# Memory attention by token tile: feed-forward weights split in quarters between its steps, with evictions, softmax steps and the norm's power in another order

## The chip, the cores and the metric

The kernel runs on one core of a Trainium2 chip. The metric is the device time of one execution in microseconds. Five engines work side by side, each through its own instruction stream in order: PE (TensorE, matmuls and transposes), ACT (ScalarE), DVE (VectorE), POOL (GpSimd) and SP (SyncE, which here only starts transfers). They wait for each other by semaphores.

## The reference, cut to what matters

The program computes two transformer blocks, of two layers each, on 256 tokens of 1024 features in float32. The change touches only the memory attention, which stands once in each of the two layers of the first block:

```
for layer in range(2):
    x = x + rms_norm(mixer(rms_norm(x, g[0])), g[1])
    q = rms_norm(x, g[2]) @ wq                     # 1024 -> 4 heads x 64
    k, v = rms_norm(mem) @ wk, rms_norm(mem) @ wv  # 256 memory tokens
    p = softmax(q k^T / 8)                         # 256 x 256 for each head
    x = x + rms_norm((p v) @ wo, g[3])             # 4 x 64 -> 1024
    h = rms_norm(x, g[4])
    x = x + rms_norm((silu(h @ wg) * (h @ wu)) @ wd, g[5])
```

The mixer of layer 0 is `even_mixer`, that of layer 1 `diff_mixer`.

## The kernel before

**Tiles.** The 256 tokens are two tiles of 128. A product with a weight is three matmuls of PE: each operand is held as a rounded high part and a low part (the rest), and high x high, high x low and low x high are added up (`three_products`, L689 to L691).

**Weights.** All weights pass as units of at most 128 x 2048 floats. SP loads a unit into one of six raw slots (`load`, L488), once the unit that held the slot is used up. `part` splits it: ACT rounds it (L521) into one of three high slots, waiting until the unit three places earlier is used; DVE subtracts (L504) and leaves the low part over the raw one. The query weight wq has a high buffer of its own ("own"), which may be written once its `opened` marks are set. `part` can work in one piece or in four quarters. `prepare` splits all that may be split; `trickle(n)` issues n steps of such a split, in quarters; `take` hands out the next unit and, with `ahead=False`, prepares only if that unit isn't whole yet. `may_part` decides: the unit three places earlier must have its last use in the program, and if `turn["gentle"]` is set, a count of filler steps must also have moved on since. In the memory attention no filler runs, so that count stands still.

**Order of the work.** The order on each engine is the order in which this Python code issues instructions. The mixer's output product `second_half` yields eight steps, tile 0 first. `memory_attention` takes six of them, begins the norm of x for tile 0 (`begin_norm`: `turn` transposes x on PE L1425, `split` evicts it with ACT L1442 and DVE L1449, four blocks for each half), takes the rest of the product, closes the mixer's sublayer (`ends`: multiply by the gain L1587, update x L1601), and then issues `norm.rest()`: the squares of x for tile 0 (ACT L1461), a small DVE step (L839) and the power on POOL (L844). Then, for each tile: queries (PE, evicted by DVE L2380 with the norm's factor and 1/8), their transposes (`turn_query`, PE L2393, evicted by ACT L2399), scores (PE L2418), maxima (DVE L2428), exponentials (ACT L2442), scaling (DVE L2453, L2458), transposes of the probabilities (`turn_probs`, PE L2473, evicted by ACT L2480 for head pair 0 and DVE L2487 for pair 1), values (PE L2503, evicted by ACT L2512 and DVE L2517), the output product by wo (`project`, two column halves), and `out_.leave`: squares (ACT L1545), their sum (DVE L1569), a power (POOL L1575), multiply (L1587), update of x (L1601). `ready.later` issues the transposes, squares, power and splits for tile 1's norm; its callback issues `turn_query(0)`, `scores(0)` and the maxima of tile 0 between them.

**Waits to know.** `turn_query` waits for DVE's latest count at its place in the program, `scores` for ACT's latest. `update of x` waits also for the latest issued squares of x.

**Hand-over.** The feed-forward (`ffn`) first takes its units f0 and f1 (gate and up weights of chunk 0, four of the eight blocks of 128 features each), multiplies tile 0 by f0, issues `ready.later` (transposes of tile 1 of x into four banks), multiplies tile 0 by f1, then tile 1 by both. f2 and f3 are chunk 1, f4 the first down weight. f2 may be rounded when wo is used up.

The first `take` of `ffn` is the only place where f0, f1 and f2 are split:

```
first = [take(ahead=False), take(ahead=False)]
for tt in range(TT):
    gate_up(0, first[0], 0, [tt])
    if tt == 0:
        ready.later(banks[4:8])
        prepare()
    gate_up(0, first[1], KD // 2, [tt])
    hidden(0, [tt])
```

## Time and profile before

| | us |
|---|---|
| median of 3 runs | 2139.26 |
| lowest, highest | 2136.69, 2139.48 |
| the profiled execution | 2141.67 |
| its span, first to last instruction | 2139.4 |
| PE busy in the span | 2039.1 (95%) |
| DVE busy | 1253.2 (59%) |
| ACT busy | 1044.2 (49%) |
| POOL busy | 140.7 (7%) |

All moments in the text are microseconds from the start of the span. The memory attention of layer 0 and the hand-over to its feed-forward lie between about 225 and 290, those of layer 1 between about 592 and 655. Matmuls are pipelined: the start of one follows the start of the last by less than its own duration.

### The profile page before, as it was taken

To read this page: it belongs to the slowest core of one execution; us is meant where nothing else is said; L and a number is where in the kernel's file an instruction comes from. 1 tells how busy PE (TensorE), PEld (TensorE's weight loads), DVE (VectorE), ACT (ScalarE), POOL (GpSimd) and SP (SyncE) were. 2 spreads that over 40 slices of the span, in tenths; PEclk is the share of its full clock that TensorE was granted. 3 is DMA by queue.
4 is the path that set the end of the run, shared out by engine and by line. 5 is a ranking of instruction groups with operands and counts; after the bars stand their busy time and mean duration, and the time that the engine had idled before them with its cause. 6 is when DMAs were issued, how large, how long until landed. Compare 5 with 4: busy or idle time off the path is not lost.

```text
span 2139.4 us, 26939 instructions
## 1 busy us (share of the span) xinstructions
PE 2039.1 (95%) x9980; PEld 1680.7 (79%) x9980; DVE 1253.2 (59%) x1872; ACT 1044.2 (49%) x1679; POOL 140.7 (7%) x146
## 2 busy tenths in 40 slices
PE   7988789999869999999999999999999999999999
PEld 7775678887758888888777788888888877878887
DVE  5546554566754556555675865545545685876444
ACT  5545454355544345444456555444443566555433
POOL 0000000000000000000312210000000221120000
PEclk9987899999989999999999999999999999999999
DMA  8430355554225555565553545555555553435552
GB/s 286 133 110 22 109 181 184 190 187 158 89 89 168 187 188 176 186 195 180 165 178 104 168 138 177 191 184 182 191 188 186 165 186 126 158 118 177 188 186 98
DMA packets 247127, 346.11 MB, mean 162 GB/s; under 512 B 26132, under 2 KB 180056, under 8 KB 247000
## 3 DMA queue, kind: packets, MB, share of 16 engines
q1 hardware_dynamic: 246168, 342.92, 49.5%
q8 instruction: 81, 1.33, 0.3%
q0 software_dynamic: 544, 1.29, 0.2%
q14 instruction: 46, 0.38, 0.1%
q10 hardware_dynamic: 288, 0.21, 0.0%
HBM read 343.32 MB, written 2.33 MB: 162 GB/s over the span
## 4 chain that ended last, share of the span: by engine, by line
PE 87%; DVE 6%; ACT 3%; issue 3%; POOL 1%; DMA 0%; ACTq 0%; DVEq 0%; POOLq 0%
PE bank L689 26%; PE bank L691 25%; PE bank L690 25%; PE bank L965 2%; DVE w_lo L504 2%; PE bank L1285 1%; ACT w_hi L521 1%; PE bank L624 1%; PE bank L1093 1%; PE bank L1425 1%; POOL gain L2659 1%; PE bank L2084 1%; PE bank L1143 1%; DVE probs L1078 1%; DVE jobstat L1012 0%
## 5 line engine op out<-in xcount | busy, mean ns | idle before, releaser
L504 DVE TENSOR_TENSOR w_lo<-raw,w_hi 128x2048 fp32r<-128x2048 f32 (+6 forms) x487 | 740.0, 1539 | 418.0 <-ACT w_hi L521 417.9
L689 PE MATMUL bank<-w_hi,h_hi 128*128 128x512 f32 (+3 forms) x1872 | 739.9, 395 | 30.2 <-DVE w_lo L504 20.4
L521 ACT CAST w_hi<-raw 128x2048 fp32r<-128x2048 f32 (+6 forms) x487 | 616.4, 1295 | 258.3 <-PE bank L691 256.8
L690 PE MATMUL bank<-w_lo,h_hi 128*128 128x512 f32 (+3 forms) x1904 | 734.3, 386 | 0.0
L691 PE MATMUL bank<-w_hi,h_lo 128*128 128x512 f32 (+3 forms) x1872 | 725.2, 387 | 0.0
L689 PEld LDWEIGHTS bank<-w_hi,h_hi 128*128 128x128 f32 x1872 | 355.9, 190 | 103.6 <-DVE w_lo L504 15.9
L690 PEld LDWEIGHTS bank<-w_lo,h_hi 128*128 128x128 f32 x1904 | 363.3, 191 | 64.1
L691 PEld LDWEIGHTS bank<-w_hi,h_lo 128*128 128x128 f32 x1872 | 355.3, 190 | 69.8
L689 PE MATMUL bank<-w_hi,ff_hi 128*128 128x512 f32 x528 | 206.4, 391 | 0.0
L691 PE MATMUL bank<-w_hi,ff_lo 128*128 128x512 f32 x528 | 205.6, 389 | 0.0
L690 PE MATMUL bank<-w_lo,ff_hi 128*128 128x512 f32 x528 | 205.5, 389 | 0.0
L1264 ACT ACTIVATE ff_silu<-bank,rs 128x256 f32<-128x256 f32 x132 | 56.4, 474 | 203.9 <-PE bank L691 203.8
L1296 ACT CAST ff_hi<-bank 128x512 fp32r<-128x512 f32 x66 | 38.8, 587 | 226.9 <-PE bank L1285 226.9
L1301 DVE TENSOR_TENSOR ff_lo<-bank,ff_hi 128x512 fp32r<-128x512 f32 x66 | 45.6, 691 | 121.5 <-ACT ff_hi L1296 121.5
L689 PEld LDWEIGHTS bank<-w_hi,ff_hi 128*128 128x128 f32 x528 | 99.1, 188 | 20.9 <-DVE ff_lo L1301 0.3
L691 PEld LDWEIGHTS bank<-w_hi,ff_lo 128*128 128x128 f32 x528 | 99.1, 188 | 20.8
L690 PEld LDWEIGHTS bank<-w_lo,ff_hi 128*128 128x128 f32 x528 | 99.1, 188 | 20.2
L1273 DVE SCALAR_TENSOR_TENSOR ff_hid<-bank,rs,ff_silu 128x256 f32<-128x256 f32 x132 | 58.4, 480 | 93.6 <-ACT ff_silu L1264 93.6
L844 POOL TENSOR_TENSOR rs<-rs,const 128x1 f32<-128x1 f32 (+3 forms) x39 | 36.0, 923 | 898.6 <-DVE rs L839 809.5
L1442 ACT ACTIVATE h_hi<-bank,cols 128x128 fp32r<-128x128 f32 x192 | 53.1, 383 | 38.5 <-PE bank L1425 38.4
L1449 DVE SCALAR_TENSOR_TENSOR h_lo<-bank,cols,h_hi 128x128 fp32r<-128x128 f32 x192 | 52.8, 344 | 15.3 <-ACT h_hi L1442 14.9
L965 PE MATMUL bank<-kT,qT 64*128 64x256 f32 (+1 forms) x320 | 44.9, 419 | 10.9 <-POOL gain L2659 7.9
(324 smaller groups left out, 1690.9 us busy)
## 6 DMA issues: line engine op xcount, KB each, us to landing
raw<-in_ffn_w SPq DMA_DIRECT2D x176, 512.0 KB, 4.7
raw<-in_w_in SPq DMA_DIRECT2D x48, 1024.0 KB, 5.3
raw<-in_ffn_w SPq DMA_DIRECT2D x44, 1024.0 KB, 4.9
raw<-in_ffn_wg SPq DMA_DIRECT2D x44, 512.0 KB, 4.0
raw<-in_ffn_wu SPq DMA_DIRECT2D x44, 512.0 KB, 5.0
raw<-in_ffn_wd SPq DMA_DIRECT2D x22, 1024.0 KB, 4.9
raw<-in_od_w_in SPq DMA_DIRECT2D x12, 1024.0 KB, 5.2
raw<-in_w_out SPq DMA_DIRECT2D x8, 1024.0 KB, 5.1
```

Of the source, the lines that this page charges most:

```text
L504: dve.tensor_tensor(lo_[:, cs], raw_[:, cs], hi[:, cs].bitcast(F32), ALU.subtract).then_inc(*dve_did.up())
L521: act.copy(hi[:, cs], raw_[:, cs]).then_inc(*act_did.up())
L689: pe.matmul(out, x_hi, u.hi[:, k, cols_], start=start, stop=False)
L690: pe.matmul(out, x_hi, u.lo[:, k, cols_], start=False, stop=False)
L691: return pe.matmul(out, x_lo, u.hi[:, k, cols_], start=False, stop=stop)
L965: mm = pe.matmul(tile(i, j, tt), l, r, start=(m == 0 and (tt == 0 or not masked)), stop=(m == len(pairs[j]) - 1 and not masked), skip_grou ...
L1264: act.activation(ff_silu[:, c % 2, tt, :], bank.t[:, 0:FF_CHUNK], ACT.Silu, scale=r(tt)).then_inc(*act_did.up())
L1273: dve.scalar_tensor_tensor(ff_hid[:, c % 2, tt, :], bank.t[:, FF_CHUNK:2 * FF_CHUNK], r(tt), ff_silu[:, c % 2, tt, :], ALU.mult, ALU.mult) ...
L1296: act.copy(ff_hi[:, c % 2, :, :], ps).then_inc(*act_did.up())
L1301: dve.tensor_tensor(ff_lo[:, c % 2, :, :], ps, ff_hi[:, c % 2, :, :].bitcast(F32), ALU.subtract).then_inc(*dve_did.up())
L1442: act.activation(h_hi[:, k0 + b, ts_], bank.t[:, b * P:(b + 1) * P], ACT.Copy, scale=gains[b]).then_inc(*act_did.up())
L1449: dve.scalar_tensor_tensor(h_lo[:, k0 + b, ts_], bank.t[:, b * P:(b + 1) * P], gains[b], h_hi[:, k0 + b, ts_].bitcast(F32), ALU.mult, ALU. ...
```

## The change

The query factor 1/8 moves from the eviction of the queries to the eviction of their transposes. For tile 0 these two evictions change engines (ACT, then DVE). `turn_query` and `scores` wait for the eviction that they need. Tile 1's transposes and scores are issued before tile 0's scaling and transposed probabilities. Four `trickle(2)` stand between the steps and `gentle` is no longer set. Both norms' `rest()` (squares and power of tile 0) are issued before the last steps of the product ahead of them. The last product of wo (`project(1, 512)`) is issued after both splits of tile 0. In layer 1, wq may be split only after the transposes of the mixer's second half. Whole diff:

```
@@ -2339,7 +2339,6 @@
             written(1)
             while "half" not in there:
                 fill()
-            own_units[1].opened = attended["o"]
             acc = out_banks()
             first_half = out_steps(acc, h_in, 0, there["half"])
             for _ in norm_steps(1):
@@ -2348,6 +2347,7 @@
             groups, steps = half_of_o(KD // 2, there["normed", 1], lambda b: cols[:, 1, c:c + 1])
             for _ in steps:
                 pass
+            own_units[1].opened = attended["o"]
             memory_keys(1)
             for _ in first_half:
                 pass
@@ -2360,7 +2360,7 @@
             W = MEM_H * HD
             PAIRS = MEM_H // 2
             kv = memory_kv[l]
-            scored, peaked, exped, scaled, copied, summed = ({} for _ in range(6))
+            queried, turned_q, scored, peaked, exped, scaled, copied, summed = ({} for _ in range(8))
             banks_of, turned_in = {}, {}
 
             def p_of(tt, j, hp):
@@ -2372,37 +2372,54 @@
                 return z[:, tt, 512 + j * 512:1024 + j * 512]
 
             def query(tt, c, n, bank, full):
+
+                if tt == 0:
+                    @block.scalar
+                    def _(act):
+                        act.wait_ge(*full)
+                        act.wait_ge(*turn["normed"][tt])
+                        act.activation(z[:, tt, 0:W], bank.t[:, 0:W], ACT.Copy, scale=rs[:, tt:tt + 1]).then_inc(
+                            *act_did.up())
+                    queried[tt] = bank.drained = act_did.now()
+                    return
 
                 @block.vector
                 def _(dve):
                     dve.wait_ge(*full)
                     dve.wait_ge(*turn["normed"][tt])
-                    dve.tensor_scalar(z[:, tt, 0:W], bank.t[:, 0:W], rs[:, tt:tt + 1], HD ** -0.5, ALU.mult,
+                    dve.tensor_scalar(z[:, tt, 0:W], bank.t[:, 0:W], rs[:, tt:tt + 1], None,
                                       ALU.mult).then_inc(*dve_did.up())
-                bank.drained = dve_did.now()
+                queried[tt] = bank.drained = dve_did.now()
 
             def turn_query(tt):
 
-                bank, ready_q, ts_ = next_bank(), dve_did.now(), slice(tt * P, (tt + 1) * P)
+                bank, ts_ = next_bank(), slice(tt * P, (tt + 1) * P)
 
                 @block.tensor
                 def _(pe):
                     pe.wait_ge(*bank.drained)
-                    pe.wait_ge(*ready_q)
+                    pe.wait_ge(*queried[tt])
                     for b in range(PAIRS):
                         m = pe.transpose(bank.t[:, b * P:(b + 1) * P], z[:, tt, b * P:(b + 1) * P], ident)
                     m.then_inc(*pe_did.up())
-
-                @block.scalar
-                def _(act):
-                    act.wait_ge(*pe_did.now())
-                    act.copy(qT[:, 0:PAIRS, ts_],
-                             bank.t[:, 0:W].rearrange("p (a b) -> p a b", a=PAIRS)).then_inc(*act_did.up())
-                bank.drained = act_did.now()
+                ps = bank.t[:, 0:W].rearrange("p (a b) -> p a b", a=PAIRS)
+                if tt == 0:
+                    @block.vector
+                    def _(dve):
+                        dve.wait_ge(*pe_did.now())
+                        dve.tensor_scalar(qT[:, 0:PAIRS, ts_], ps, HD ** -0.5, None, ALU.mult).then_inc(*dve_did.up())
+                    bank.drained = dve_did.now()
+                else:
+                    @block.scalar
+                    def _(act):
+                        act.wait_ge(*pe_did.now())
+                        act.activation(qT[:, 0:PAIRS, ts_], ps, ACT.Copy, scale=HD ** -0.5).then_inc(*act_did.up())
+                    bank.drained = act_did.now()
+                turned_q[tt] = bank.drained
 
             def scores(tt):
 
-                there, ts_ = act_did.now(), slice(tt * P, (tt + 1) * P)
+                ts_ = slice(tt * P, (tt + 1) * P)
                 for j in range(2):
                     banks_of[tt, j] = next_bank()
                     banks_of[tt, j].held = True
@@ -2411,7 +2428,7 @@
                 def _(pe):
                     pe.wait_ge(*banks_of[tt, 0].drained)
                     pe.wait_ge(*banks_of[tt, 1].drained)
-                    pe.wait_ge(*there)
+                    pe.wait_ge(*turned_q[tt])
                     for hp in range(PAIRS):
                         for j in range(2):
                             r_ = slice(j * HD, (j + 1) * HD)
@@ -2543,12 +2560,12 @@
             norm.turn()
             norm.split(0)
             norm.split(1)
+            ready = norm.rest()
             for _ in products:
                 pass
             for end in ends:
                 end()
             ends.clear()
-            ready = norm.rest()
             wq = take(ahead=False)
             pair = [next_bank() for _ in range(TT)]
             for bank in pair:
@@ -2569,46 +2586,44 @@
             queries(1)
             powers(0, 0)
             powers(0, 1)
+            turn_query(1)
             normalise(0, 0)
-            turn_query(1)
             normalise(0, 1)
+            scores(1)
+            trickle(2)
             turn_probs(0, 0)
-            scores(1)
+            peak(1, 0)
             turn_probs(0, 1)
-            peak(1, 0)
             peak(1, 1)
             powers(1, 0)
+            values(0)
             powers(1, 1)
-            turn["gentle"] = True
-            trickle()
-            values(0)
             normalise(1, 0)
             normalise(1, 1)
             turn_probs(1, 0)
-            turn_probs(1, 1)
+            trickle(2)
             for bank in banks[4:8]:
                 bank.held = True
             out_ = Sublayer(post_gain)
-            turn["gentle"] = False
             wo = take(ahead=False)
-            turn["gentle"] = True
             project(0, 0)
-            trickle()
+            turn_probs(1, 1)
+            trickle(2)
             project(0, 512)
             values(1)
-            trickle()
+            trickle(2)
             project(1, 0)
             norm = begin_norm(x, col_of[("pre", l, 4)], rs[:, 0:2])
             norm.turn()
             norm.split(0)
+            norm.split(1)
+            ready = norm.rest()
             project(1, 512)
             for end in ends:
                 end()
             ends.clear()
-            norm.split(1)
-            turn["gentle"] = False
             attended["o"] = marks()
-            return norm.rest()
+            return ready
 
         for l in range(DEPTH):
             products = (even_mixer if l % 2 == 0 else diff_mixer)(load_gain(a["sandwich_g"][l, 1, :]))
```

## Rows read from the trace of the kernel before

**Rows 1.** page, busy time over the span; then windows: PE, PEld, DVE, ACT, POOL, clock, DMA

```profile
PE 2039.1 (95%) x9980; PEld 1680.7 (79%) x9980; DVE 1253.2 (59%) x1872; ACT 1044.2 (49%) x1679; POOL 140.7 (7%) x146
...
292.00:345.00 53.00, 53.00 (x244) 43.85 (x243) 28.14 (x21) 21.82 (x20) 0.00 (x0) 1.00 0.57 180
```

**Rows 2.** timeline of the hand-over in layer 0 (start, duration, engine, line, operation)

```profile
266.31 0.60 ACT L1545 ACTIVATE sq<-bank 128x512 f32<-128x512 f32 x1 [1.41 <-PE bank L691]
...
267.89 1.42 DVE L1601 SCALAR_TENSOR_TENSOR x<-o_buf,stat,x 128x512 f32<-128x512 f32 x2
...
268.93 5.52 ACT L521 CAST w_hi<-raw 128x2048 fp32r<-128x2048 f32 x3
...
270.88 6.70 DVE L504 TENSOR_TENSOR w_lo<-raw,w_hi 128x2048 fp32r<-128x2048 f32 x3 [0.28 <-ACT w_hi L521]
...
273.27 0.76 PE L689 MATMUL bank<-w_hi,h_hi 128*128 128x512 f32 x1 [7.01 <-DVE w_lo L504]
...
278.50 1.03 PE L1425 MATMUL bank<-const,x 128*128 128x128 f32 x8
...
287.74 0.37 SPq L488 DMA_DIRECT2D raw<-in_ffn_wd  x1
```

**Rows 3.** waits from 594 to 640, the same place in layer 1

```profile
PE bank L689 <- DVE w_lo L504: 7.0, 1, 7.0
```

**Rows 4.** timeline of layer 0, from the norm to the first output product

```profile
232.68 0.48 DVE L2380 TENSOR_SCALAR z<-bank,rs 128x256 f32<-128x256 f32 x1 [0.74 <-POOL rs L844]
...
233.57 0.41 PE L2393 MATMUL bank<-const,z 128*128 128x128 f32 x2 [1.12 <-DVE rs L839]
...
234.53 1.13 PE L2418 MATMUL bank<-kT,qT 64*128 64x256 f32 x8 [0.55 <-ACT qT L2399]
...
239.52 0.48 DVE L2380 TENSOR_SCALAR z<-bank,rs 128x256 f32<-128x256 f32 x1 [1.21 <-PE bank L691]
...
242.48 1.13 PE L2418 MATMUL bank<-kT,qT 64*128 64x256 f32 x8 [0.77 <-ACT z L2480]
...
249.09 1.94 PE L2473 MATMUL bank<-const,probs 128*128 128x128 f32 x8 [2.91 <-DVE jobstat L2453]
...
251.81 0.80 PE L689 MATMUL bank<-w_hi,h_hi 128*128 128x512 f32 x1 [0.78 <-DVE z L2487]
...
260.77 0.47 PE L689 MATMUL bank<-w_hi,h_hi 128*128 128x512 f32 x1 [2.11 <-issue]
```

**Rows 5.** groups by form over the whole run: busy, mean ns | idle before

```profile
L521 ACT CAST w_hi<-raw 128x2048 fp32r<-128x2048 f32 x243 | 464.0, 1915 | 199.3 <-PE bank L691 199.3
L521 ACT CAST w_hi<-raw 128x512 fp32r<-128x512 f32 x196 | 112.8, 624 | 52.8 <-PE bank L691 52.8
...
L504 DVE TENSOR_TENSOR w_lo<-raw,w_hi 128x2048 fp32r<-128x2048 f32 x243 | 557.8, 2300 | 352.1 <-ACT w_hi L521 352.1
L504 DVE TENSOR_TENSOR w_lo<-raw,w_hi 128x512 fp32r<-128x512 f32 x196 | 134.5, 720 | 36.1 <-ACT w_hi L521 35.9
```

**Rows 6.** timeline of layer 1: end of the mixer, first query eviction, f1 used up

```profile
579.04 2.28 DVE L504 TENSOR_TENSOR w_lo<-raw,own_hi 128x2048 fp32r<-128x2048 f32 x1
581.24 1.65 DVE L680 SCALAR_TENSOR_TENSOR h_lo<-bank,cols,h_hi 128x256 fp32r<-128x256 f32 x4
...
583.00 0.47 PE L689 MATMUL bank<-w_hi,h_hi 128*128 128x512 f32 x1 [1.40 <-issue]
...
599.32 0.48 DVE L2380 TENSOR_SCALAR z<-bank,rs 128x256 f32<-128x256 f32 x1 [0.74 <-POOL rs L844]
...
653.07 0.37 SPq L488 DMA_DIRECT2D raw<-in_ffn_wd  x1
```

**Rows 7.** windows of layer 0, columns as in rows 1

```profile
247.00:249.00 2.00, 0.00 (x0) 0.00 (x0) 1.17 (x5) 0.76 (x4) 0.00 (x0) 0.68 0.00 0
249.00:257.00 8.00, 7.13 (x20) 5.40 (x20) 2.01 (x5) 1.27 (x3) 0.00 (x0) 0.50 0.00 0
...
266.00:274.00 8.00, 0.99 (x4) 0.66 (x3) 6.50 (x11) 7.70 (x11) 2.86 (x4) 0.64 0.50 151
```

More of the change, by code:

```diff
@@ L2374, in query, with _ @@
             def query(tt, c, n, bank, full):
+                if tt == 0:
+                    @block.scalar
+                    def _(act):
+                        act.wait_ge(*full)
+                        act.wait_ge(*turn["normed"][tt])
+                        act.activation(z[:, tt, 0:W], bank.t[:, 0:W], ACT.Copy, scale=rs[:, tt:tt + 1]).then_inc(
+                            *act_did.up())
+                    queried[tt] = bank.drained = act_did.now()
+                    return
                 @block.vector
@@ L2545, in memory_attention @@
             norm.split(1)
+            ready = norm.rest()
             for _ in products:
@@ L2571, in memory_attention @@
             powers(0, 1)
+            turn_query(1)
             normalise(0, 0)
-            turn_query(1)
             normalise(0, 1)
+            scores(1)
+            trickle(2)
             turn_probs(0, 0)
-            scores(1)
+            peak(1, 0)
             turn_probs(0, 1)
-            peak(1, 0)
             peak(1, 1)
             powers(1, 0)
+            values(0)
             powers(1, 1)
-            turn["gentle"] = True
-            trickle()
-            values(0)
             normalise(1, 0)
@@ L2591, in memory_attention @@
             out_ = Sublayer(post_gain)
[L2592 removed]
             wo = take(ahead=False)
[L2594 removed]
             project(0, 0)
[L2596 removed]
+            turn_probs(1, 1)
+            trickle(2)
             project(0, 512)
             values(1)
[L2599 removed]
+            trickle(2)
             project(1, 0)
@@ L2603, in memory_attention @@
             norm.split(0)
+            norm.split(1)
+            ready = norm.rest()
             project(1, 512)
@@ L2607, in memory_attention @@
             ends.clear()
-            norm.split(1)
-            turn["gentle"] = False
             attended["o"] = marks()
-            return norm.rest()
+            return ready
         for l in range(DEPTH):
```

43 lines of the change are left out of this document (23 added, 20 removed).

## The prediction, made before the changed kernel ran

> **What bounds the kernel now.** I read the page first: PE is busy 95% of the span, so time can only come from PE's idle stretches and from stretches at a low clock. In the feed-forward that follows the memory attention PE is busy 53.00 of 53 us at clock 1.00 [rows 1]: whatever the attention gains is passed on whole, and nothing can be gained there. Then the waits: the longest single wait of PE in each of the two layers is the same one, 7.0 us at the hand-over, until DVE has written a low part [rows 2, 3]. The timeline shows why. The last output product ends at 266.3. Only then are f0, f1 and f2 split, in whole units and behind the squares of x: ACT starts at 268.93, DVE at 270.88, PE at 273.27 [rows 2]. Last the timeline of the attention itself: a chain passes from PE to ACT or DVE and back, with idle PE between [rows 4], and PE's clock falls in it: 0.68 and 0.50 after the idle stretch at 247 to 249, again 0.64 around the 7 us wait [rows 7]. 12 matmuls take 5.2 us there (273.27 to 278.50) and 36 take 8.3 at clock 1.00 (279.4 to 287.7) [rows 2], so 0.43 and 0.23 each. These are the levels of 1.2 and 2.4 GHz.
>
> **The change part by part, layer 0.** I follow one chain with durations of the rows, first at clock 1.00.
>
> *Norm's power and queries.* The squares of tile 0 move ahead of the mixer's last square, into an idle ACT; their DVE and POOL steps move with them. Tile 0's query eviction waited 0.74 for POOL [rows 4]; now ACT does it when PE is done, at 231.7. Its transposes waited 1.12 for the small DVE step of tile 1 [rows 4]; they no longer do, but their eviction, now on DVE, stands behind that same step (233.4). So the first scores start at 233.8, not at 234.53, and tile 1's query eviction at 238.8, not at 239.52: 0.7 gained. Moving the factor 1/8 costs nothing: the same number of instructions on the same shapes.
>
> *Tile 1's scores.* They started at 242.48 because two copies of tile 0's probabilities and the scaling stood before them [rows 4]. Now: eviction to 239.3, transposes to 239.8, copy to 240.2, scores at 240.3. 2.2 gained in all. The next work on ACT, two quarter casts, lies in its wait for PE.
>
> *To the first output product.* From scores(1) to it went 9.3 us (242.48 to 251.81): maxima, all four exponential steps, values, the scaling, and then transposes of both head pairs (1.94) and a copy on DVE before the product could start [rows 4]. Now values(0) stands between the exponentials and the product follows the first transposes of tile 1: scores 1.1, transposes of tile 0's second head pair and their copy 1.7, values 1.2, their evictions 0.85, scaling of tile 1's first pair 0.75, its transposes 0.5, signals included: 6.1. The product starts at about 246.3, 5.5 earlier. Its bank may be one that ACT still reads until 247.1; I charge 0.8 for that.
>
> *The quarters.* A quarter cast takes 624 ns against 1915 for a whole one, a quarter low part 720 against 2300 [rows 5]. So f0 and f1 cost 8 x 0.62 = 5.0 us of ACT and 8 x 0.72 = 5.8 of DVE, one DVE quarter of it after the attention. The Trainium skill, VectorE: DVE Perf Modes, section "The TRN2 errata", speaks against splitting: instructions that read SBUF pay a fixed extra each on ScalarE and VectorE. The rows agree: four quarters cost 0.58 us of both engines more for a unit than one whole piece (2.50 - 1.92, 2.88 - 2.30) [rows 5]. On ACT all eight stand before idle time. On DVE three stand in front of the x update of tile 0 and tile 1's low values, so the idle before project(1, 0), 2.11 now [rows 4], grows to 2.9. No DMA moves but by its slot's release: f0 and f1 are in their slots before the attention.
>
> *The two orders of the last product.* project(1, 512) now ends at 257.8 instead of 266.3, 8.5 earlier (5.5 from before, 4.8 from 24 matmuls at 0.23 instead of 0.43, minus the 0.8 of longer idle and 1.0 of new short waits, for the square behind quarters and the transposes of x). What is newly late: its squares stand on ACT behind tile 0's second split and the norm's squares, 259.6 instead of 257.9. They hold the sum, POOL's power, the multiply and tile 1's update of x, there at 262.6, and so PE's transposes of tile 1.
>
> *Hand-over.* f0 is whole, so PE multiplies tile 0 at 258.8, after the split of tile 0's first half, to 261.8; waits 0.9 for x; transposes to 263.7; f1 (its last quarter done at 263.2) to 266.5; f2's four quarters stand before tile 1's splits on DVE, costing 0.5; both units for tile 1 to 272.7. Now that point is 287.7 [rows 2]. **15.0 us gained.** f2 is needed only then and is whole by 265.7.
>
> **Layer 1.** Its first query eviction is at 599.32, 366.64 after layer 0's; f1 is used up at 653.07 [rows 6], 286.4 on layer 0's scale, so 13.7 gained. Besides, the low part of wq (2.28) stands before the mixer's last h_lo, for which PE waits 1.40 [rows 6]. It moves behind: the h_lo is there at 580.8, before PE asks, **1.4 gained**. wq and wo are then whole about 10 us before use.
>
> **Sum.** At clock 1.00 throughout: 15.0 + 13.7 + 1.4 = 30.1. But by the same chain the new order still has idle stretches of PE (1.8 before 246, 2.9 before 254, 1.2 and 0.9 at the hand-over). If the clock stays low from 247.6 to 262, about as long as now [rows 7], f1 is used up at 276.3, 3.6 later in each layer: 22.9. What the new order's clock does no row shows; I take the middle, 26.5, since the longest idle shrinks only from 2.91 to about 2.9, in another place, while the one of 7.01 goes. Minus 2 x 0.8 for the bank: **24.9**. The ends: 30.1, and 11.5 with the clock low until f1 is through (below). The profiled execution took 2141.67, 2.4 more than the median of the runs, 2139.26; the sum is a difference within its span and I take it off the median: 2139.3 - 24.9 = **2114.4**.
>
> **Rivals.**
> - *Only the hand-over gains.* The quarters fill what the new order frees, and the last product ends at 266.3 as now. Then x of tile 1 comes 1.8 later than now (271.1), transposes end at 272.2 instead of 279.5: 7.3 each, 2 x 7.3 + 1.4 = 16.0, 2123. For: both engines carry the work and are strictly in order. Against: ACT is busy 1.27 of the 8 us from 249 to 257, DVE 2.01 [rows 7].
> - *The clock stays low through f0 and f1.* f1 is used up at 282.0: 5.7 + 4.4 + 1.4 = 11.5, 2127.8. For: it is low now after idle stretches, 0.50 from 249 to 257 with PE busy 7.13 of 8 us [rows 7]. The Trainium skill, TensorE: Matmul & The Clock Gate, section "What's actually happening", says that the throttled state is the default and activity releases it; by that rule a denser attention loses less clock than the present one, which would give a time nearer to 2109. The trace agrees so far that the clock is 1.00 throughout the dense feed-forward [rows 1].
> - *Slower: the quarters lie on the chain.* Seven DVE and eight ACT quarters fall where PE waits, each delaying the next step of the softmax: 5.0 + 5.0 = 10.0 us a layer, against 7.3 at the hand-over. 2 x 2.7 - 1.4 = 4.0 slower, 2143. It decides once more than 7.3 of 10.0 us is exposed and reordering gives nothing. Against it: before project(1, 0) only three DVE quarters can stand in the way, and ACT waits for PE elsewhere.
> - *The splits aren't issued.* If a unit weren't allowed by its predecessor's use, trickle would do nothing and the 7 us wait stay; the attention's reordering alone would give about 6 a layer, 2126. Against: f0's and f1's predecessors are the mixer's last two units, used before, and `gentle`, which forbade them, is off.
>
> **Chances.** Forecast 0.64, hand-over only 0.16, low clock 0.08, not issued 0.05, slower 0.04, none of these 0.03. All but the last two are faster by more than 0.2% (4.3 us, about what a measurement of this kernel can tell from no change): faster 0.92, same 0.04, slower 0.04. Range: from 2106, the 30.1 with 3 us for stretches elsewhere whose clock may fall otherwise once all is shifted, to 2127, which takes in the hand-over case and part of the low clock one.
>
> **What would show it.** Right: no cast or low part of 128x2048 at the hand-over but eight quarter casts a layer inside the attention and four after it; PE's wait for L504 at f0 gone and one of about 1 us for tile 1's x in its place; scores(1) about 2 us after tile 1's query eviction began, not 3; the first output product some 13 to 14 us after the first query eviction, not 19; layer 1's 1.40 gone. Wrong: a wait of PE on a low value behind quarters longer than 4 us before project(1, 0); clock 0.50 at f0; a whole split still at the hand-over; idle of PE in the feed-forward, where the gain would be given back.

## The result, and the profile after

The changed kernel takes 2111.01 us (median of 4 runs, 2110.32 to 2112.74) against 2139.01 of the kernel before beside it: ratio 0.9872, 95% interval [0.9855, 0.9890], 28.0 us less. The forecast was 2114.4, its range 2106 to 2127.

Two executions, one of e2 below (8310.19 us) and one of the kernel before beside e5 to e8 (7141.30), lie thousands of microseconds above the rest, and no reading uses them.

The spans of the two profiled executions, 2139.4 and 2108.4, differ by 31.0, three more than the medians: the profiled execution of before (2141.67) took 2.7 us more than the median beside it, that of the changed kernel (2110.32) 0.7 less. Most of this lies in one place outside the change, shown at the end.

The page of the changed kernel, busy time over the span (as rows 1): PE has 10.9 us less busy time with the same 9980 matmuls, so part of the gain is clock; DVE and ACT have 18 instructions more each.

```profile
PE 2028.2 (96%) x9980; PEld 1672.0 (79%) x9980; DVE 1253.8 (59%) x1890; ACT 1043.8 (50%) x1697; POOL 140.5 (7%) x146
```

Groups by form of the changed kernel (as rows 5): six units, f0, f1 and f2 of each layer, have gone from whole pieces to quarters (243 to 237, 196 to 220). The four quarters still cost 0.59 us of ACT (4 x 625 - 1913) and 0.54 of DVE (4 x 709 - 2296) more than the whole.

```profile
L504 DVE TENSOR_TENSOR w_lo<-raw,w_hi 128x2048 fp32r<-128x2048 f32 x237 | 543.3, 2296 | 350.3 <-ACT w_hi L521 350.3
L521 ACT CAST w_hi<-raw 128x2048 fp32r<-128x2048 f32 x237 | 452.5, 1913 | 199.6 <-PE bank L691 199.6
...
L504 DVE TENSOR_TENSOR w_lo<-raw,w_hi 128x512 fp32r<-128x512 f32 x220 | 148.6, 709 | 36.9 <-ACT w_hi L521 36.6
L521 ACT CAST w_hi<-raw 128x512 fp32r<-128x512 f32 x220 | 126.1, 625 | 52.3 <-PE bank L691 52.3
```

The timeline of the changed kernel, first the attention of layer 0 (as rows 4), then its hand-over (as rows 2), then layer 1 (as rows 6). Line numbers have moved: L2381 and L2390 are the query evictions of tiles 0 and 1 (before L2380), L2403 their transposes (L2393), L2410 and L2416 the evictions of these, L2435 the scores (L2418), L2470 the scaling (L2453), L2490 the transposes of the probabilities (L2473), L2534 the low part of the values (L2517).

```profile
232.37 0.47 ACT L2381 ACTIVATE z<-bank,rs 128x256 f32<-128x256 f32 x1 [2.19 <-PE bank L691]
...
234.54 1.13 PE L2435 MATMUL bank<-kT,qT 64*128 64x256 f32 x8 [1.06 <-DVE qT L2410]
...
239.24 0.48 DVE L2390 TENSOR_SCALAR z<-bank,rs 128x256 f32<-128x256 f32 x1 [1.21 <-PE bank L691]
...
240.60 1.13 ACT L521 CAST w_hi<-raw 128x512 fp32r<-128x512 f32 x2
...
240.85 1.14 PE L2435 MATMUL bank<-kT,qT 64*128 64x256 f32 x8 [0.56 <-ACT qT L2416]
...
246.71 1.09 PE L2490 MATMUL bank<-const,probs 128*128 128x128 f32 x4 [1.73 <-DVE jobstat L2470]
...
247.45 0.78 PE L689 MATMUL bank<-w_hi,h_hi 128*128 128x512 f32 x1
...
254.14 0.16 DVE L1569 SCALAR_TENSOR_TENSOR stat<-stat 128x1 f32<-128x1 f32 x1 [0.54 <-ACT sq L1545]
...
255.00 1.42 DVE L1601 SCALAR_TENSOR_TENSOR x<-o_buf,stat,x 128x512 f32<-128x512 f32 x2
256.33 0.42 DVE L2534 TENSOR_TENSOR h_lo<-bank,h_hi 128x256 fp32r<-128x256 f32 x1
...
256.85 0.47 PE L689 MATMUL bank<-w_hi,h_hi 128*128 128x512 f32 x1 [2.44 <-ACT w_hi L521]
...
261.09 1.12 ACT L1461 ACTIVATE sq<-x 128x1024 f32<-128x1024 f32 x1
...
262.13 0.66 ACT L1545 ACTIVATE sq<-bank 128x512 f32<-128x512 f32 x1
...
262.70 2.24 ACT L521 CAST w_hi<-raw 128x512 fp32r<-128x512 f32 x4
...
263.77 1.42 DVE L1601 SCALAR_TENSOR_TENSOR x<-o_buf,stat,x 128x512 f32<-128x512 f32 x2
...
264.67 1.29 PE L1425 MATMUL bank<-const,x 128*128 128x128 f32 x8 [1.10 <-DVE x L1601]
...
265.10 3.09 DVE L504 TENSOR_TENSOR w_lo<-raw,w_hi 128x512 fp32r<-128x512 f32 x5
...
274.59 0.37 SPq L488 DMA_DIRECT2D raw<-in_ffn_wd  x1
...
566.06 1.66 DVE L680 SCALAR_TENSOR_TENSOR h_lo<-bank,cols,h_hi 128x256 fp32r<-128x256 f32 x4
...
568.90 2.29 DVE L504 TENSOR_TENSOR w_lo<-raw,own_hi 128x2048 fp32r<-128x2048 f32 x1 [1.19 <-ACT own_hi L521]
```

PE no longer stops 7.0 us for a low part. f1 is used up at 274.59 instead of 287.74. No cast of 128x2048 is left at the hand-over: eight quarter casts lie inside the attention (the two shown at 240.60, and two each at 248.31, 250.98 and 254.72) and four behind it, at 262.70. In layer 1 the low part of wq now follows the mixer's last h_lo instead of standing before it.

Windows of the changed kernel, layer 0 and one later stage (columns as in rows 1): the clock still falls in the attention, but it is back at 1.00 for f0 and f1, where before it was 0.64 [rows 7].

```profile
247.00:252.00 5.00, 5.00 (x17) 4.12 (x16) 2.46 (x6) 3.23 (x7) 0.00 (x0) 0.50 0.00 0
252.00:257.00 5.00, 2.56 (x22) 1.78 (x21) 4.37 (x9) 2.20 (x6) 0.55 (x1) 0.92 0.00 0
...
262.00:270.00 8.00, 6.86 (x32) 4.96 (x32) 7.16 (x18) 7.80 (x20) 2.86 (x4) 1.00 0.85 241
...
280.00:330.00 50.00, 50.00 (x227) 41.42 (x226) 26.63 (x19) 20.83 (x18) 0.00 (x0) 1.00 0.58 190
...
1849.00:1853.00 4.00, 4.00 (x24) 3.40 (x23) 4.00 (x8) 2.98 (x6) 2.69 (x2) 1.00 0.25 98
```

In layer 1 it falls twice: it is 0.70 from 598 to 603, 1.00 in the next 4 us and 0.60 from 607 to 611.

**Where the time went.** I cut each trace at the same instructions. Attention: from the mixer's third square to the first square of the attention's own output product. Product: from there to its last square. Hand-over: from there to the second silu, when f1 is used up. Wq: in layer 1, from the last reduction of the mixer's norm to the mixer's third square. Differences of starts in the timelines, in us; the span is that of the traced execution, the median that of all (e11 is one execution):

| kernel | attention, layers 0, 1 | product | hand-over | wq | span | median |
|---|---|---|---|---|---|---|
| before | 29.9, 31.2 | 11.5, 9.0 | 21.4, 21.4 | 21.2 | 2139.4 | 2139.0 |
| changed | 24.7, 24.5 | 11.7, 11.9 | 12.5, 12.5 | 19.5 | 2108.4 | 2111.0 |
| e1 only the order | 23.1, 23.1 | 10.8, 10.9 | 19.3, 19.2 | 19.6 | 2115.8 | 2122.2 |
| e11 only the quarters | 30.8, 32.1 | 11.5, 9.1 | 13.7, 13.7 | 21.2 | 2125.0 | 2126.9 |
| e3 wq back | 23.7, 23.6 | 12.1, 12.4 | 12.5, 12.5 | 21.2 | 2109.1 | 2112.1 |
| e4 old front | 26.0, 26.0 | 11.1, 11.1 | 12.5, 12.5 | 19.5 | 2110.9 | 2115.0 |
| e10 old back | 27.0, 26.4 | 10.5, 10.5 | 12.5, 12.5 | 19.6 | 2111.0 | 2112.9 |
| e12 old front and back | 29.8, 30.6 | 10.9, 10.5 | 12.5, 12.5 | 19.5 | 2119.7 | 2119.2 |
| e5 casts twice | 24.7, 24.7 | 12.3, 12.5 | 12.5, 12.5 | 19.6 | 2109.9 | 2111.7 |
| e6 low parts twice | 24.7, 24.2 | 13.7, 13.6 | 12.4, 12.5 | 19.6 | 2114.4 | 2115.6 |
| e7 whole units | 27.6, 27.9 | 14.0, 13.0 | 12.0, 12.0 | 19.5 | 2117.9 | 2122.0 |
| e8 late rest | 23.6, 24.7 | 11.4, 10.4 | 13.7, 13.7 | 19.5 | 2108.5 | 2110.5 |
| e9 late rest, x sooner | 24.4, 24.5 | 8.2, 8.2 | 12.5, 12.4 | 19.5 | 2104.4 | 2104.7 |

In the feed-forward PE is busy 50.00 of 50 us, as before [rows 1], so nothing of the gain is given back there. The hand-over gave 9.0 and 8.9, the attention with its product 5.0 and 3.8, the mixer's end in layer 1 1.7: 28.4. The span shows 2.6 more, from stretches the change doesn't touch: 3.6 behind the second hand-over, less 1.0 ahead of the two attentions.

**How far two traces can be compared.** Layer 0 of e3 has the same instructions as layer 0 of the changed kernel, for e3 differs from it in layer 1 only. It took 48.2 us where the changed kernel took 48.9, with the attention 1.1 shorter and the product 0.4 longer. The cause is the clock, as the last section shows. So a difference of 0.7 us a layer between two traces is no more than one code shows by itself. And a traced execution needn't be a typical one: the time of an execution is 1.9 to 2.4 us above its span; so the trace of e1 is of its fastest execution, 4.1 below its median, that of e4 lies 2.3 below, and that of e12 is of its slowest, 2.5 above.

### The profile page after: what moved, and what is told of

It reads as the page before. It is cut to its first block and busy times, and to the rows that moved or that the text cites. A ratio compares the mean times of both kernels' runs of the same rounds, so it can differ in the third digit from the quotient of the medians.

```text
span 2108.4 us, 26993 instructions
## 1 busy us (share of the span) xinstructions
PE 2028.2 (96%) x9980; PEld 1672.0 (79%) x9980; DVE 1253.8 (59%) x1890; ACT 1043.8 (50%) x1697; POOL 140.5 (7%) x146
## 5 line engine op out<-in xcount | busy, mean ns | idle before, releaser
L689 PE MATMUL bank<-w_hi,h_hi 128*128 128x512 f32 (+3 forms) x1872 | 738.3, 394 | 12.1 <-DVE w_lo L504 4.7
L965 PE MATMUL bank<-kT,qT 64*128 64x256 f32 (+1 forms) x320 | 43.8, 411 | 10.9 <-POOL gain L2674 7.9
```

The lines of the kernel that those rows point to most:

```text
L689: pe.matmul(out, x_hi, u.hi[:, k, cols_], start=start, stop=False)
L965: mm = pe.matmul(tile(i, j, tt), l, r, start=(m == 0 and (tt == 0 or not masked)), stop=(m == len(pairs[j]) - 1 and not masked), skip_grou ...
```

## The experiments

### The two halves of the change

Only the order: the four `trickle(2)` are gone, and f0, f1 and f2 are split at the hand-over as before.

```
             scores(1)
-            trickle(2)
             turn_probs(0, 0)
...
             values(1)
-            trickle(2)
             project(1, 0)
```

> The changed kernel without its four trickle(2): f0, f1 and f2 are split whole at the hand-over again, everything else is the new order. If pre-splitting and order are both worth something (my theory): the last output product ends at about the same time as in the changed kernel, then PE waits some 6 us for f0's low part and has a low clock after it, about 7 us a layer more than the changed kernel's 2111: 2125, half of the whole gain. If the order is worth nothing and all of the gain is the hand-over (rival 1): 2137 or so, the layer-1 gain of the moved wq alone. If the order and the clock carry nearly all (rival 2): 2113 to 2116.

Measured: 2122.15 (2118.06 to 2122.83), ratio 0.9914 [0.9899, 0.9928]. The wait for the low part is back, 5.33 long; the timeline of e1:

```profile
259.42 5.49 ACT L521 CAST w_hi<-raw 128x2048 fp32r<-128x2048 f32 x3
...
261.74 4.49 DVE L504 TENSOR_TENSOR w_lo<-raw,w_hi 128x2048 fp32r<-128x2048 f32 x2
264.13 0.77 PE L689 MATMUL bank<-w_hi,h_hi 128*128 128x512 f32 x1 [5.33 <-DVE w_lo L504]
```

Only the quarters: the kernel before, with the four `trickle(2)` at the same steps in its own order.

```
             scores(1)
+            trickle(2)
...
-            turn["gentle"] = True
-            trickle()
             values(0)
...
             values(1)
-            trickle()
+            trickle(2)
```

> The kernel before with only the four trickle(2) put between its old steps and gentle left off: the quarters alone, in the old order. My theory: PE's 7.0 us wait goes and a wait of about 3 us for tile 1's x remains (its update ends 3 us after the product); 7 to 9 us a layer gained less 1 for quarters on the chain: 2139 - 15 = 2124. Rival 1: 2113 to 2116, since the hand-over is all. Rival 2, or quarters that lie on the old chain: 2132 or more.

Measured: 2128.03 (2127.22 to 2128.09), ratio 0.9944 [0.9927, 0.9960]. The trace comes from one more execution of the same kernel:

> The quarters alone in the old order once more, for its trace: from the first output product to f1 used up. If quarters lie on the old chain, the attention up to the first product is longer than the 29.9 us of before by 1 to 2 us, and the hand-over shorter by 8 to 9.

That execution took 2126.89. Its PE waits between 226 and 290:

```profile
PE bank L689 <- DVE z L2487: 1.7, 1, 1.7
PE bank L689 <- DVE w_lo L504: 1.2, 1, 1.2
```

The 7.0 has become 1.2: f1's last quarter stands on DVE behind the norm. The expectation (2124) had 4 us more of gain. In exchange the copy L2487, for which PE waited 0.78 before the first output product [rows 4], stands behind a low quarter, and PE waits 1.7: in the old order a quarter lies on the chain.

**What follows.** The order alone gains 17.4 (2139.5 - 2122.15), the quarters alone 11.5 (2139.5 - 2128.03). Together they would give 28.9, and the changed kernel gains 28.0. By the medians the change has two nearly independent halves, of 60 and 40%. The rival that only the hand-over gains falls, and so does the opposite reading, that the quarters are worth nothing beside the order.

### Parts of the order

Wq's early split restored:

```
             while "half" not in there:
                 fill()
+            own_units[1].opened = attended["o"]
             acc = out_banks()
...
-            own_units[1].opened = attended["o"]
             memory_keys(1)
```

> The changed kernel with the query weights of layer 1 allowed to be split where they were before. Theory: DVE does wq's 2.28 us low part before the mixer's last h_lo again, PE waits 1.4 us, 1.4 to 1.7 us slower than 2111.0: 2112.6. Rival: the wait is made up by the attention's own waits for ACT and DVE, no difference: 2111.

Measured: 2112.06 (2111.05 to 2112.95), ratio 0.9872 [0.9855, 0.9888]. It is 1.05 above the changed kernel, which the medians can't tell from nothing; the trace can: the stretch at the mixer's end is 21.21 long instead of 19.53, and the wait is back between 560 and 600:

```profile
PE bank L689 <- issue: 1.4, 1, 1.4
```

The 1.7 are real, once in the program.

The old front: `query`, `turn_query` and `scores` as before, with their waits, and the old order up to scores(1).

```
-            turn_query(1)
             normalise(0, 0)
+            turn_query(1)
             normalise(0, 1)
+            turn_probs(0, 0)
             scores(1)
             trickle(2)
-            turn_probs(0, 0)
             peak(1, 0)
```

> The changed kernel with the old queries, transposes and scores (both query evictions on DVE with the factor 1/8, the old waits) and the old order of tile 1's transposes and scores; the quarters, the norm's power and everything after stay new. Theory: scores of tile 1 start 2.2 us later in each layer and the rest follows: 4.4 slower, 2115.4. Rival: the front has slack, the first output product waits for something else: under 1 us, 2111 to 2112.

Measured: 2115.04 (2112.10 to 2119.52), ratio 0.9886 [0.9870, 0.9902]. The median is 4.0 above the changed kernel, close to the 4.4 expected. The traced execution, 2112.78, was one of its shorter ones and shows less. In it scores(1) starts at 242.48, counted from the mixer's third square 2.1 later than in the changed kernel, and the attention is 1.3 and 1.5 longer, but the product is 0.6 and 0.8 shorter. Net 0.7 a layer in this trace, where 2.2 was expected. Whether the front is worth 4 us or 1.5 stays open: its four executions spread over 7.4, and only a short one was traced.

The old back: values(0) behind all exponentials, and tile 1's transposes of both head pairs together.

```
             powers(1, 0)
-            values(0)
             powers(1, 1)
+            values(0)
             normalise(1, 0)
             normalise(1, 1)
             turn_probs(1, 0)
+            turn_probs(1, 1)
             trickle(2)
...
             project(0, 0)
-            turn_probs(1, 1)
```

> The changed kernel with the old order in the attention's second half: values of tile 0 after both exponential steps, and the transposes of tile 1's second head pair before project(0, 0), which shares their bank with a DVE copy. Front, quarters and hand-over stay new. Theory: the first output product waits for those transposes (1.0 us at the low clock) and the copy (0.7) and for values(0): 2 to 3 us a layer slower, 2115 to 2117. Rival: what stands before the product only moves behind it: under 1 us, 2111 to 2112.

Measured: 2112.87 (2111.75 to 2115.47), ratio 0.9877 [0.9864, 0.9891]. The first output product starts at 250.18, the attention is 2.3 and 1.9 longer, but the product gets 1.2 and 1.4 back, for the second transposes no longer stand inside it. Net 1.0 and 0.5, where 2 to 3 a layer was expected.

So single parts were worth 1.9 to 4.0 by the medians, while the order as a whole was worth 17. The last run takes front and back together:

```
-            turn_query(1)
             normalise(0, 0)
+            turn_query(1)
             normalise(0, 1)
+            turn_probs(0, 0)
             scores(1)
...
-            values(0)
             powers(1, 1)
+            values(0)
...
             turn_probs(1, 0)
+            turn_probs(1, 1)
             trickle(2)
```

> The changed kernel with both halves of the softmax order of before at once: its evictions and waits of queries and transposes and its order up to scores(1) (the front), and values(0) behind all exponentials and both transposes of tile 1 together (the back). Kept are the quarters, the earlier rest of both norms, the later wq and the last product behind both splits. The front alone cost 0.7 a layer in the trace, the back alone 0.5 to 1.0, and the kernel with only the quarters on the old order stands 16 us above the changed one. Theory that the parts add up: 2 to 4 us above the changed kernel, 2113 to 2115, and nearly all of the 16 us then lies in what is kept here. Theory that each half covers the other (a wait saved in one is worth nothing while the other stands): more than 6 us above it, 2117 to 2122, with the time from the mixer's end to the first output product back near 26 to 27 us, PE's clock low before project(0, 0), and the last square of the attention late.

Measured: 2119.15 (2115.78 to 2121.61), ratio 0.9900 [0.9883, 0.9916], 8.1 above the changed kernel. Windows of e12, in layer 1:

```profile
587.00:592.00 5.00, 3.64 (x30) 2.93 (x28) 2.50 (x8) 2.61 (x8) 0.58 (x2) 1.00 0.59 203
599.00:603.00 4.00, 3.12 (x14) 2.06 (x16) 2.37 (x4) 1.91 (x6) 0.00 (x0) 0.52 0.65 264
603.00:608.00 5.00, 3.27 (x23) 2.88 (x24) 2.10 (x8) 1.70 (x6) 0.00 (x0) 0.50 0.01 3
```

and its timeline:

```profile
599.00 1.94 PE L2418 MATMUL bank<-kT,qT 64*128 64x256 f32 x8 [0.77 <-ACT z L2480]
...
609.29 0.80 PE L689 MATMUL bank<-w_hi,h_hi 128*128 128x512 f32 x1 [0.78 <-DVE z L2487]
```

**What follows.** In the traces the front costs 1.4 over both layers and the back 1.6, together they cost 8.8. But these compare a short execution of e4 with the longest of e12, and part of the excess is the clock: here scores(1) and everything up to the first output product run at 0.50, the scores take 1.94 instead of 1.13. In layer 0 of the same execution 1.2 of the 4.2 us is only the clock in `queries(1)` (0.66 from 236 to 241, where e4 has 1.00; from scores(0) to scores(1) it takes 9.13, where e4 takes 7.95 with the same instructions in the same order). By the medians it is 4.0 for the front, 1.9 for the back and 8.1 for both: an excess of 2.2, less than the 7.4 over which e4's own runs spread. That the two halves together cost about 8 is shown. That they cost more than the sum of their parts, each covering part of the other, is not shown.

What is left of the order is for the most part the difference of e2 and e12: the earlier rest of both norms, the place of the last product and wq. It is 8.9 by the medians, 6.1 in the segments of the two traces: 1.7 of wq, 1.3 a layer at the hand-over, 1.1 and 1.6 in the attention, and in the product 0.7 gained in layer 0 but 1.4 lost in layer 1. The 1.1 and 1.6 aren't all order, for the two kernels also place one trickle differently: e2 has it between `turn_probs(1, 0)` and `turn_probs(1, 1)`, where PE waits 1.7 for the copy, e12 behind both, where PE waits 0.78 as before the change. These parts weren't tried one by one.

### What the quarters cost

Each quarter cast of the attention a second time, into memory that is unused there:

```
+                    if turn["doubled"]:
+                        n_, to_ = spare(act)
+                        act.copy(to_, raw_[:, cs]).then_inc(*act_did.up())
+                        spare_marks[n_] = act_did.now()
                     act.copy(hi[:, cs], raw_[:, cs]).then_inc(*act_did.up())
```

> The changed kernel with each of the eight quarter casts a layer in the attention preceded by a second one of the same size on ACT, into unused memory: 8 x 0.53 to 0.62 = 4.2 to 5 us of ACT added a layer. If the quarters lie in ACT's idle time (theory): at most 1.5 us a layer slower, 2111 to 2114. If they lie on the chain (the slower rival's mechanism): 8 to 10 us slower, 2119 to 2121.

Measured: 2111.68 (2110.42 to 2113.41), ratio 0.9875 [0.9859, 0.9890]. Eight more casts, 5.0 us of ACT a layer, cost 0.6 and 0.8 a layer in the trace, no more than two traces of one code differ by, and nothing that the median shows. On ACT the quarters are nearly all hidden.

The low parts in the same way:

```
                     dve.wait_ge(*rounded)
+                    if turn["doubled"]:
+                        n_, to_ = spare(dve)
+                        dve.tensor_tensor(to_, raw_[:, cs], hi[:, cs].bitcast(F32), ALU.subtract).then_inc(
+                            *dve_did.up())
+                        spare_marks[n_] = dve_did.now()
```

> The changed kernel with seven extra low-part subtractions of a quarter a layer on DVE, one in front of each of the first seven, into unused memory: 7 x 0.62 to 0.72 = 4.3 to 5 us of DVE added a layer. My forecast had three DVE quarters in front of tile 0's x update on the chain: then 2 us a layer slower, and one more in front of the maxima 0.6: 2116. If all are hidden: 2111 to 2112. If all are exposed: 2120 or more.

Measured: 2115.64 (2114.45 to 2116.33), ratio 0.9891 [0.9873, 0.9908]. Seven more low parts, 5.0 us of DVE, cost 1.9 and 1.7 a layer in the product and nothing in the attention. The doubled low parts are exposed before `project(1, 0)`, where the forecast had expected it.

What the single ones cost can be read at equal clock: up to 252 PE runs at 1.00 in layer 0 of e1, which has no quarters, and of e3, which has them. The attention is 23.1 and 23.7, for in e3 the first square stands behind two quarter casts, and PE's wait before `project(1, 0)` is 2.02 and 2.57, for the sum stands behind two low parts. So the quarters cost 0.6 and 0.5 us a layer there, 1.1 of the about 10 us that they keep the two engines busy.

The same two units in whole pieces, one behind scores(1) and one behind `turn_probs(1, 1)`; f2 is whole again too:

```
             scores(1)
-            trickle(2)
+            whole_split()
...
-            trickle(2)
+            whole_split()
             project(0, 512)
             values(1)
-            trickle(2)
```

> The changed kernel with f0 split as one whole piece where its first two quarters stood and f1 as one whole piece where the fifth and sixth stood; f2 then comes after tile 1's norm work. Same work, fewer instructions (0.6 us less on each engine for a unit). If quartering matters (theory): DVE's 2.3 us piece stands in front of tile 1's maxima, ACT's 1.9 in front of the copy of probabilities, 2.5 to 3.5 us a layer slower: 2117. If only the place of the split matters, not its size: 2110 to 2111.

Measured: 2122.00 (2120.31 to 2122.78), ratio 0.9921 [0.9906, 0.9937]. 11.0 above the changed kernel, where 6 was expected. The segments show 8.7 of it, 4.7 and 4.0 a layer, and the traced execution has a lower mean clock, 0.976 against 0.981. The timeline of e7, whose lines stand six further (L2451 are the maxima, L695 is PE's high product):

```profile
242.01 2.29 DVE L504 TENSOR_TENSOR w_lo<-raw,w_hi 128x2048 fp32r<-128x2048 f32 x1 [1.35 <-ACT w_hi L521]
...
244.22 0.68 DVE L2451 TENSOR_REDUCE jobstat<-bank 128x2 f32<-128x512 f32 x1
...
255.23 2.29 DVE L504 TENSOR_TENSOR w_lo<-raw,w_hi 128x2048 fp32r<-128x2048 f32 x1 [0.51 <-ACT w_hi L521]
...
260.13 0.77 PE L695 MATMUL bank<-w_hi,h_hi 128*128 128x512 f32 x1 [4.17 <-issue]
```

A whole low part stands in front of the maxima, another in front of the sum and the low values, and PE waits 4.17 before `project(1, 0)` instead of 2.44. So the quarters aren't only a way to have f0 in time: moving the splits into the attention in whole pieces is worth nothing (e1, with the splits at the hand-over, takes 2122.15). The size of a piece and the number of places, two instead of four, changed together here and weren't told apart. The Trainium skill, VectorE: DVE Perf Modes, section "The TRN2 errata", says that many small pieces pay a fixed latency each where one large piece pays it once, and recommends pieces of at least 512 elements, which a quarter just has. The rows agree on the latency, 0.54 to 0.59 us a unit and engine, and these runs show what paying it buys here: 11 us for six units.

### What is late next

The last product first, then the second split and the norm's rest:

```
             norm.split(0)
-            norm.split(1)
-            ready = norm.rest()
             project(1, 512)
             for end in ends:
                 end()
             ends.clear()
+            norm.split(1)
+            ready = norm.rest()
```

> The changed kernel with project(1, 512), its squares and tile 1's x update issued before tile 0's second split and the norm's squares, as in the old order, and the quarters kept. In the changed kernel PE waits 1.1 us for tile 1's x because those squares stand on ACT behind the second split and the norm's squares (product over at 260.8, squares at 262.13). Theory: x of tile 1 comes 1.3 us earlier, f1's product for tile 0 still finds its split, 1 us a layer faster: 2109. Rival: the second split comes late for f1 and for tile 1 and gives the gain back: 2111 or more.

Measured: 2110.47 (2108.74 to 2111.69), ratio 0.9868 [0.9852, 0.9883]: no gain that can be told. The timeline of e8 has a new wait in the place of the one for x:

```profile
265.50 3.09 DVE L504 TENSOR_TENSOR w_lo<-raw,w_hi 128x512 fp32r<-128x512 f32 x5
...
266.23 0.50 PE L689 MATMUL bank<-w_hi,h_hi 128*128 128x512 f32 x1 [1.17 <-DVE w_lo L504]
```

f1's last quarter is the first of the five, and it now stands behind the second split. So in the next run the fourth trickle takes three steps, and the update of x for tile 0 is issued behind values(1), not in front of it (the sum and the multiply stay where they were):

```
+            finish, out_.finish = out_.finish, lambda tt: None
             project(0, 512)
             values(1)
-            trickle(2)
+            out_.finish = finish
+            out_.finish(0)
+            trickle(3)
             project(1, 0)
...
             norm.split(0)
-            norm.split(1)
-            ready = norm.rest()
             project(1, 512)
...
             ends.clear()
+            norm.split(1)
+            ready = norm.rest()
```

> The changed kernel with three more moves: the late rest of the run before; one more step of f1's split before project(1, 0), so that its last low part no longer stands behind the norm on DVE (that cost the late rest its gain: PE waited 1.2 us for it instead of 1.1 for x); and values(1) with its low part issued before the update of x for tile 0, for which project(1, 0) now waits 2.4 us on PE. Theory: project(1, 0) starts 1.4 us earlier, tile 1's x 1.3 earlier, and nothing else is late: 1.5 to 2 us a layer, 2107 to 2108. Rival: the split of the second half, needed by f1's product, becomes the bound at the hand-over: 2109.5 or more.

Measured: **2104.74** (2104.34 to 2106.29), ratio 0.9838 [0.9825, 0.9852], 6.3 below the changed kernel, and more than expected. The timeline of e9:

```profile
254.71 0.41 DVE L2534 TENSOR_TENSOR h_lo<-bank,h_hi 128x256 fp32r<-128x256 f32 x1
255.04 1.40 DVE L1601 SCALAR_TENSOR_TENSOR x<-o_buf,stat,x 128x512 f32<-128x512 f32 x2
255.23 0.47 PE L689 MATMUL bank<-w_hi,h_hi 128*128 128x512 f32 x1 [1.06 <-ACT w_hi L521]
256.37 1.89 DVE L504 TENSOR_TENSOR w_lo<-raw,w_hi 128x512 fp32r<-128x512 f32 x3
```

The low values come before the update of x and before the quarters. PE waits 1.06 instead of 2.44, and the product is 3.5 and 3.6 shorter. The row names ACT as the releaser in both kernels, but in the changed one that cast began at 254.72 and PE started at 256.85, behind DVE's update of x (255.00, 1.42) and the low values (256.33, 0.42): it was DVE, as moving DVE's work shows.

## Why the prediction was right, and where its sizes were off

The mechanism is the one forecast: the splits left the hand-over, the chain in the attention got shorter, and PE in the feed-forward passed the gain on whole. That the number came within 3.4 us is in part luck, since the clock term was a choice of the middle between two bounds and the term for the bank was too much.

Moments of layer 0 are compared less 0.8: the layer starts that much later in the new trace, by the third square of the mixer, in code that is the same.

**Norm's power and queries: right.** Forecast scores(0) at 233.8, measured 233.7. ACT takes tile 0's queries at 232.37, when PE is done, and PE waits 1.06 for the eviction on DVE.

**Tile 1's scores: right.** Forecast 240.3, measured 240.05, 2.4 gained.

**First output product: nearly.** Forecast 246.3, or 247.1 with the 0.8 for a bank; measured 246.65. The trace lists no wait for a bank, so the 2 x 0.8 was a term too many. The 0.35 are the clock: the four transposes ahead of the product (246.71) took 1.09, and in e3, at 1.00, they took 0.63 and the product followed them 0.38 after their start instead of 0.74. The working reads as if each step kept its gain alone. The runs leave this open: with the front undone the median is 4.0 higher, as it would be, but the one traced execution shows 0.7 a layer instead of 2.2 (e4), and the back's 1.9 by the median is less than the 2 to 3 a layer expected (e10).

**The clock: right in kind, too large.** It is 0.50 from 247 to 252, around a wait of 1.73 for the scaling (246.71), 0.92 in the next 5 us and 1.00 at f0. The forecast took half of 3.6 a layer. Measured by f1 used up: 272.7 at clock 1.00, 276.3 with a low clock, in fact 273.8; so 1.1, and in layer 1 1.0 (13.7 less 12.7). These are what is left after all other errors of the working, no measurement of the clock alone. The 1.5 too much here, the bank's 1.6 and 0.3 of wq account for 3.4 of the 3.5 by which 24.9 fell short of the segments' 28.4. The mean granted clock rose from 0.974 to 0.981. From the Trainium skill, TensorE: Matmul & The Clock Gate, section "What's actually happening", by which the throttled state is the default and activity releases it, the prediction had worked out 2109; the trace agrees in direction.

**The quarters: right.** Eight casts and seven low parts in the attention, four casts and five low parts behind it. Forecast 2.9 of idle PE before `project(1, 0)`, measured 2.44 and 2.57 (layer 1). Most of this wait is the order on DVE, which puts the update of x in front of the low values; it was there before the quarters (2.11, and 2.02 in e1). In layer 0 the quarters add nothing to it, for DVE was idle 0.54 just before the sum (254.14); in e3 and in layer 1 the sum stands directly behind two of them. E5 shows that more casts on ACT are covered, e6 that more low parts on DVE are exposed just there.

**The two orders of the last product: right.** The square of the last product stands behind the norm's squares (262.13 behind 261.09) and holds tile 1's update of x (263.77); forecast 0.9 of waiting for it, measured 1.10 in layer 0 and 0.33 in layer 1. What wasn't foreseen: removing it brings nothing (e8), since f1's last quarter is late by the same amount.

**Wq: right.** Forecast 1.4, measured 1.70, and 1.68 by e3.

**The rivals.** "Only the hand-over gains" (2123) falls: the attention and its product gave 5.0 and 3.8. "The clock stays low through f0 and f1" (2127.8) falls with 1.00 from 262 to 270. "The splits aren't issued" (2126) is the state of e1, with 2122.15: the reordering alone is worth 17.4, or 8.0 a layer beside the 1.4 of wq, more than the 6 taken for it. "Slower" (2143) needed 7.3 of 10.0 us exposed; the quarters expose 1.1 a layer (e1 against e3), doubling them 0.7 of 5.0 on ACT and 1.6 of 5.0 on DVE, and even whole units inside the attention stay 17 below the kernel before.

**The sum.** 14.0 + 12.7 + 1.7 = 28.4 in the two attentions, 28.0 between the medians.

## What to carry to other kernels

Split work that is due at a hand-over in pieces no longer than the gaps it has to fill, and look not only at what the pieces cost (0.55 us a unit on each engine) but at which instruction stands behind them on their engine: the same units in whole pieces gave back 11 us. Before a trace of a variant is read for less than a microsecond, look where its execution lies among the others, and compare one stretch whose code is the same in both: layer 0 of e3 and of the changed kernel differ by 0.7 us. When the named releaser of a wait had long been done, look at the engine whose work lies just before the waiting instruction's start: with the low values in front of the update of x, and one quarter more in the fourth trickle, the step from e8 to e9 gave 5.7 us.

## What the runs showed of the hardware that was not expected

**The clock fell in one execution and not in another, at the same code.** In a later stage that the change doesn't touch, PE waited 3.03 us in both kernels for DVE; then the kernel before, in this window, ran at 0.50, twelve transposes in 2.79 us (columns as in rows 1):

```profile
1877.00:1881.00 4.00, 4.00 (x16) 3.69 (x16) 4.00 (x9) 2.23 (x5) 2.49 (x2) 0.50 0.29 112
```

The changed kernel ran them in 1.50 at 1.00 (its window 1849:1853 above). This is most of the 3.6 us by which the rest of the program differs, and why 31.0 between the spans is 28.0 between the medians. The Trainium skill, TensorE: Matmul & The Clock Gate, section "What's actually happening", says of the start of a kernel that the number of matmuls until the clock rises differs from run to run; the traces show the like in the middle of one, here and in e12's `queries(1)`, 0.66 against 1.00 in e4. A difference of two traces of 1 or 2 us in this kernel is therefore to be read with the clock's windows beside it.

**Where the clock falls moves too.** In layer 0 of the changed kernel it fell before the first output product, in e1, with the order alone, behind it, and it would be easy to blame the quarters. But e3 runs the same instructions there, after the same wait of 1.7, and was at 1.00 in this window; these are a row of its timeline and one of its windows:

```profile
246.14 0.63 PE L2490 MATMUL bank<-const,probs 128*128 128x128 f32 x4 [1.74 <-DVE jobstat L2470]
247.00:252.00 5.00, 4.08 (x31) 2.99 (x30) 3.57 (x8) 3.73 (x9) 0.00 (x0) 1.00 0.00 0
```

In e3 the clock fell later, behind the wait of 2.57 before `project(1, 0)`: 0.78 from 252 to 257. So the instructions alone don't settle at which of the two waits the clock falls. By the start of `project(1, 0)` the early fall had cost 1.7 us (31.2 after the mixer's third square, against 29.5 in e3), and over the layer 0.7. What decides it was not found.
